# Accumulating depthwise taps in PSUM and splitting eight more gate strips, four by an adding DMA

## The chip, the cores and the metric

The kernel runs on one core of one Trainium2 chip. The metric is the device time of one execution in microseconds (us). The kernel before ran three times; one more execution was profiled.

## The reference

Two transformer-like blocks run one after the other on a sequence of 256 tokens with 1024 features, all in float32: retention and latent attention first, then a block with two mixers and a gated feed-forward part. The change lies in the mixer part of the second block:

```python
h = layer_norm(x) * (1.0 + sc1[:, None]) + sh1[:, None]
proj = h @ w_in[l]
a_val, a_gate, u_pool, gate_a, gate_b = jnp.split(
    proj, [COL_A_VAL, COL_A_GATE, COL_POOL, COL_GATE_A], axis=-1)
ya = a_val * jax.nn.sigmoid(a_gate)
ya = causal_dwconv(ya, w_dw_a[l], b_dw_a[l])          # 31 taps, 512 channels
ya = jax.nn.silu(layer_norm(ya, ln_a_g[l], ln_a_b[l]))
ya = ya @ w_pw_a[l]
pooled = causal_multiscale_pool(u_pool)               # windows 2, 4, 8, 16
...
merged = jax.nn.sigmoid(gate_a) * ya + jax.nn.sigmoid(gate_b) * yb
```

## The kernel before

**Weights and strips.** Every weight matrix is cut into blocks of 128 x 1024 (512 KB), numbered through the kernel (`B_WA` conv_in, 8 blocks; `B_WP` pool_in, 4; `B_WG` gates, 16; `B_POOL`, `B_PW` and so on). SyncE loads block b into slot b mod 4 of the ring `raw` (L337 to L373). A block that gives 128 output features for all 256 tokens is called a strip.

**Two ways to multiply.** A *split* strip needs two float32r copies of the block: the high part `whi`, a copy by ACT (`split`, L959 to L971), and the low part `wlo` = raw - whi, a subtract by VectorE (`split`, L1488 to L1495). Both work three blocks ahead of the call (`AHEAD`), and count up `hi_done` and `lo_done`. TensorE then makes three float32r products for each of eight 128 x 128 tiles (`products`, L469 to L481): high by high, high by low, low by high. A *native* strip (`plain_tokens`, L507) is multiplied in float32 straight from `raw`, with no copies; ACT and VectorE then raise `hi_done` and `lo_done` by a bare count (`skip_split`, L1040 and L1610), and SyncE waits for TensorE to be done with the slot (`load_plain`, `load_plain_loop`).

**The stage around the change.** TensorE runs conv_in (eight strips, three native and five split), pool_in (0 and 1 split, 2 and 3 native), gate strips 0 to 11 native, the matmul with ones for the convolution's mean (`conv_mean`, L596), then gate strips 12 to 15 split, with the matmul for its variance behind 13 (L902 to L920). Results of two strips share a bank: `GA[0]`, `GA[1]` in turn, evacuated by ACT with a sigmoid (`evac`, L1126). After the gates come the pooling product, the pointwise product of the convolution branch and the mixing product.

**The depthwise convolution** is VectorE's (L1966 to L2023). The gated values go into `CI`, four tiles of 128 channels with 30 zeros in front. Tap k of tile c is one `scalar_tensor_tensor` over 256 tokens: `CO[c] = CI[c, k:k+256] * w + CO[c]`, both tiles in SBUF; the first tap is a `tensor_scalar` with the bias. Each tap waits for the one before it in its tile (semaphore `conv_tap[c]`). 26 taps (four of them first taps) stand between the conv_in splits, 98 in a loop of seven passes of 14 taps. Two adds then form the channel sums (`CS`) for `conv_mean`; VectorE next makes the low parts of gate strips 12 and 13 and centres the result.

**The pooling** is GpSimd's (L2301 to L2312): once all four pool_in strips are evacuated into `U`, four windows one after the other, a few adds and two scalings each; ACT copies the result as a high part (L1372) behind a wait for all four.

The order of the work is written out by hand on every engine; each engine follows its own list, and semaphores tie them together.

Of the kernel before, what the change touches and what calls it, by code (L numbers as in the profile page):

```python
# [24 lines left out]
ALU = mybir.AluOpType  # L25
# [7 lines left out]
RING = 4  # L33
# [39 lines left out]
B_WP = B_WA + 8  # L73
# [11 lines left out]


KEPT = [B_PG0 + 4 + j for j in range(4)]


def raw_count(b):  # L90
# [34 lines left out]
def program(nc, x_in, pre_in, p_in, pos_in, cols_in, rows_in, mask_in, tri_in, cnt_in, ident_in, bias_in, ada_in, w, out):  # L125

    ctx = ExitStack()
    with ctx:
# [3 lines left out]
        def sem(name):  # L132
            return ctx.enter_context(nc.semaphore(name))
# [86 lines left out]
        bank = [PB[i // 2][:, 512 * (i % 2):512 * (i % 2) + 512] for i in range(8)]  # L220
        GA, GD = bank[0:2], bank[2:4]
        M0, M1, M2, M3 = bank[4:8]


        raw_loaded = [sem(f"raw_loaded{s}") for s in range(RING)]
        lo_done, hi_done, pe_done = sem("lo_done"), sem("hi_done"), sem("pe_done")
        act_free, dve_free = sem("act_free"), sem("dve_free")
        ada_loaded = [sem(f"ada_loaded{s}") for s in range(2)]
        plain_a, plain_d = sem("plain_a"), sem("plain_d")
        spare_loaded = [sem(f"spare_loaded{s}") for s in range(6)]  # L230
# [105 lines left out]
        def _(sp):  # L336
# [24 lines left out]
                    sp.wait_ge(pe_done, base + j + 1)  # L361
                    load(base + j, w[name][j], 1024)

            def load_plain_loop(base, name, count, per):

                with sp.Fori(0, count) as i:
                    for j in range(per):
                        sp.wait_ge(pe_done, base + j + 1 + per * i)
                        load(base + j, w[name][bass.ds(per * i + j, 1)].rearrange("b p n -> p (b n)"), 1024, per, i)

            def load_all(base, name):
                load_some(base, name, 0, w[name].shape[0])
# [70 lines left out]
            load_plain(B_WA, "conv_in", 6, 7)  # L443
            load_some(B_WA, "conv_in", 7, 8)
            load_all(B_WP, "pool_in")
            load_plain_loop(B_WG, "gates", 4, 4)
            load_all(B_POOL, "pool_w")
            load_all(B_PW, "pw")
            load_all(B_WO, "mix")
# [16 lines left out]
        def _(pe):  # L466
            mm = nc.tensor.matmul

            def products(base, parts, per=0, i=0, before=()):  # L469


                s = base % RING
                pe.wait_ge(lo_done, base + RING + 1 + per * i)
                for n, (t, a, o, start, stop) in enumerate(parts):
                    if n < len(before) and before[n]:
                        pe.wait_ge(*before[n])
                    c = slice(t * P, t * P + P)
                    mm(o, whi[:, s, c], a[:, 0, :], start=start, stop=False)  # L478
                    mm(o, whi[:, s, c], a[:, 1, :], start=False, stop=False)  # L479
                    last = mm(o, wlo[:, s, c], a[:, 0, :], start=False, stop=stop)  # L480
                last.then_inc(pe_done, 1)  # L481
# [38 lines left out]
            def free_a(k, per=0, i=0):  # L520

                pe.wait_ge(act_free, k + 1 + per * i)
                return GA[k % 2]
# [378 lines left out]
            for j in range(4):  # L902
# [3 lines left out]
                    strip(B_WP + j, halves(b)[j % 2], H)  # L906
                else:
                    plain_tokens(B_WP + j, halves(b)[j % 2])
            with pe.Fori(0, 3) as i:
                for j in range(4):  # L910
                    if j % 2 == 0:
                        b = free_a(A_WG + j // 2, 2, i)
                    plain_tokens(B_WG + j, halves(b)[j % 2], 4, i)
            conv_mean()
            for j in range(12, 16):
                if j % 2 == 0:
                    b = free_a(A_WG + j // 2)
                strip(B_WG + j, halves(b)[j % 2], H)
                if j == 13:
                    conv_squares()  # L920
            pe.wait_ge(pooled_ready, 1)
# [34 lines left out]
        def _(act):  # L956
            activation = nc.scalar.activation

            def split(base, n=1024, per=0, i=0):  # L959

                b = base + AHEAD
                if b >= B_END:
                    return
                s = b % RING
                if b in SPARE:
                    act.wait_ge(spare_loaded[SPARE[b]], spare_count(b))
                else:
                    act.wait_ge(raw_loaded[s], raw_count(b) + 16 * (per // RING) * i)
                if b not in KEPT:
                    act.wait_ge(pe_done, used_first(b) + per * i)  # L970
                activation(parts_of(b, n)[0], block_in(b, n), ACT.Copy).then_inc(hi_done, 1)  # L971

            def used(base, per=0, i=0):

# [62 lines left out]
                act.wait_ge(done, n)  # L1037
                activation(H[:, 4 * q:4 * q + 4, 0, tok(t)], zt[:, 4 * q:4 * q + 4, :], ACT.Copy).then_inc(turn_hi, 1)

            def skip_split(n):  # L1040

                activation(warm[:, 15:16], ones[:, 0:1], ACT.Copy).then_inc(hi_done, n)

            def dyn(a, t, n):
                return a[:, bass.ds(t, n), :]
# [314 lines left out]
            split(B_WA + 5)  # L1360
            value_gate(2)
            split(B_WA + 6)
            skip_split(14)
            value_gate(3)
            act.wait_ge(pads, 1)

            evac(B_WP + 1, 0, U[:, 0:2, 16:16 + T], ACT.Copy)
            evac(B_WP + 3, 1, U[:, 2:4, 16:16 + T], ACT.Copy)
            with act.Fori(0, 2) as i:
                evac(B_WG + 1, 0, dyn(G, 4 * i, 2), ACT.Sigmoid, 4, i)  # L1370
                evac(B_WG + 3, 1, dyn(G, 4 * i + 2, 2), ACT.Sigmoid, 4, i)
            act.wait_ge(pooled, 4)  # L1372
            activation(Sh, PO, ACT.Copy).then_inc(pooled_hi, 1)
            evac(B_WG + 9, 0, pair(G, 4), ACT.Sigmoid)
            for j in range(9, 12):
                split(B_WG + j)
# [106 lines left out]
        def _(dve):  # L1483
# [488 lines left out]
            def taps(c, ks, i=0, per=0):  # L1972

                for k in ks:
                    x = CI[:, c, bass.ds(k + per * i, T)]
                    w_tap = dcol("dwa", CONV_K * c + k + per * i)
                    if per == 0 and k == 0:
                        dve.wait_ge(dve_free, V_WA + c + 3)
                        ts(CO[:, c, :], x, w_tap, col("bdwa", c), ALU.mult, ALU.add).then_inc(conv_tap[c], 1)
                    else:  # L1980
                        dve.wait_ge(conv_tap[c], k + per * i)
                        stt(CO[:, c, :], x, w_tap, CO[:, c, :], ALU.mult, ALU.add).then_inc(conv_tap[c], 1)  # L1982

            split(B_WA)
            gated_value(0)
# [15 lines left out]
                taps(1, (3 + k,))  # L2001
                taps(2, (k,))
            split(B_WA + 6)
            skip_split(14)
            taps(0, (9,))
            for k in range(5, 10):
                taps(1, (k,))
# [1 line left out]
                    taps(2, (2,))  # L2009
            gated_value(3)  # L2010
            taps(3, (0, 1, 2))
            with dve.Fori(0, 7) as i:
                for k in range(4):
                    if k < 3:
                        taps(0, (10 + k,), i, 3)
                        taps(1, (10 + k,), i, 3)
                    taps(2, (3 + k,), i, 4)
                    taps(3, (3 + k,), i, 4)
            for c in range(4):
                dve.wait_ge(conv_tap[c], CONV_K)  # L2020
            tt(CS, pair(CO, 0), pair(CO, 1), ALU.add).then_inc(conv_sum, 1)
# [189 lines left out]
        def _(pool):  # L2211
# [86 lines left out]
            nc.gpsimd.memset(U[:, :, 0:16], 0.0).then_inc(pads, 1)  # L2298
            pool.wait_ge(pads, 1)

            pool.wait_ge(act_free, A_WP + 2 + 2)  # L2301
            for g, window in enumerate(WINDOWS):
                src, shift, n = U[:, g, :], 1, 0
                while shift < window:
                    lo = 2 * shift - 1
                    dst = W1[:, n % 2, :]
                    chained(gtt(dst[:, lo:16 + T], src[:, lo:16 + T], src[:, lo - shift:16 + T - shift], ALU.add))
                    src, shift, n = dst, 2 * shift, n + 1
                chained(gtt(src[:, 16:32], src[:, 16:32], cnt[:, g, :], ALU.mult))
                chained(gts(src[:, 16:16 + T], src[:, 16:16 + T], 1.0 / window, None, ALU.mult))  # L2310
                gtt(PO[:, g, :], src[:, 16:16 + T], U[:, g, 16:16 + T], ALU.subtract).then_inc(pooled, 1)
                pool.wait_ge(pooled, g + 1)  # L2312
# [123 lines left out]
```

## Time and profile before

| | us |
|---|---|
| median of 3 runs | 845.52 (844.92 to 847.47) |
| the profiled execution | 846.33 |
| its span in the profile | 844.5 |
| TensorE busy in the span | 831.2 |
| VectorE busy | 667.9 |
| ACT busy | 454.9 |
| GpSimd busy | 48.7 |

The span runs from the first to the last instruction; the execution's time is 1.83 us longer. Matmuls overlap, so that TensorE's busy time says where it worked, not how fast. Durations of neighbouring VectorE or ACT instructions overlap a little as well: the time from start to start is what such an instruction costs in a row of them. The granted TensorE clock was 1.00 in all stretches from 520 to 640 us.

### The profile page before, as it was taken

To read this page: it belongs to the slowest core of one execution; us is meant where nothing else is said; L and a number is where in the kernel's file an instruction comes from. 1 tells how busy PE (TensorE), PEld (TensorE's weight loads), DVE (VectorE), ACT (ScalarE), POOL (GpSimd) and SP (SyncE) were. 2 spreads that over 40 slices of the span, in tenths; PEclk is the share of its full clock that TensorE was granted. 3 is DMA by queue.
4 is the path that set the end of the run, shared out by engine and by line. 5 is a ranking of instruction groups with operands and counts; after the bars stand their busy time and mean duration, and the time that the engine had idled before them with its cause. 6 is when DMAs were issued, how large, how long until landed. Compare 5 with 4: busy or idle time off the path is not lost.

```text
span 844.5 us, 15113 instructions
## 1 busy us (share of the span) xinstructions
PE 831.2 (98%) x5434; PEld 759.5 (90%) x5434; DVE 667.9 (79%) x982; ACT 454.9 (54%) x680; POOL 48.7 (6%) x61
## 2 busy tenths in 40 slices
PE   9999999999999999999999999999999999999995
PEld 9899999988878999999988889988988999999884
DVE  7979888686966887787866777999898888788566
ACT  6464545554646665657555536102853867777440
POOL 0009000000012000000000000060000000000000
PEclk9999999999999999999999999999999999999998
DMA  7857565679634747383648562444662565566541
GB/s 271 303 196 246 204 243 200 223 252 379 226 102 162 263 137 264 114 286 124 243 149 329 196 224 97 133 152 157 219 219 99 199 204 188 179 193 229 187 164 50
DMA packets 48141, 168.98 MB, mean 200 GB/s; under 512 B 5602, under 2 KB 6242, under 8 KB 48100
## 3 DMA queue, kind: packets, MB, share of 16 engines
q1 hardware_dynamic: 40324, 142.18, 49.6%
q10 hardware_dynamic: 7776, 26.25, 8.7%
q8 instruction: 26, 0.43, 0.2%
q14 instruction: 15, 0.12, 0.0%
HBM read 167.36 MB, written 1.05 MB: 199 GB/s over the span
## 4 chain that ended last, share of the span: by engine, by line
PE 85%; DVE 8%; issue 3%; ACT 2%; DMA 1%; DVEq 1%; ACTq 0%
PE bank L478 13%; PE bank L479 12%; PE bank L480 12%; PE bank L545 9%; PE bank L547 9%; PE bank L546 9%; DVE WK L1982 4%; PE bank L491 3%; PE bank L696 2%; PE bank L697 2%; PE bank L698 2%; PE bank L588 1%; DVE wlo L1495 1%; PE bank L819 1%; PE bank L837 1%
## 5 line engine op out<-in xcount | busy, mean ns | idle before, releaser
L971 ACT ACTIVATE whi<-raw 128x1024 fp32r<-128x1024 f32 (+1 forms) x232 | 240.1, 1040 | 218.3 <-PE bank L480 95.3
L1495 DVE TENSOR_TENSOR wlo<-raw,whi 128x1024 fp32r<-128x1024 f32 (+1 forms) x232 | 278.5, 1212 | 79.7 <-ACT whi L971 77.1
L478 PE MATMUL bank<-H,whi 128*128 128x256 f32 x784 | 224.5, 286 | 0.5 <-DVE wlo L1495 0.5
L480 PE MATMUL bank<-H,wlo 128*128 128x256 f32 x784 | 221.8, 283 | 0.0
L479 PE MATMUL bank<-H,whi 128*128 128x256 f32 x784 | 221.7, 283 | 0.0
L478 PEld LDWEIGHTS bank<-H,whi 128*128 128x128 f32 x784 | 150.3, 192 | 1.8 <-issue 1.7
L479 PEld LDWEIGHTS bank<-H,whi 128*128 128x128 f32 x784 | 150.4, 192 | 0.1
L480 PEld LDWEIGHTS bank<-H,wlo 128*128 128x128 f32 x784 | 150.3, 192 | 0.0
L545 PE MATMUL bank<-whi,Y 128*128 128x512 f32 x216 | 84.3, 390 | 0.0
L547 PE MATMUL bank<-whi,Y 128*128 128x512 f32 x216 | 84.1, 389 | 0.0
L546 PE MATMUL bank<-wlo,Y 128*128 128x512 f32 x216 | 84.1, 389 | 0.0
L1511 DVE SCALAR_TENSOR_TENSOR ada_acc<-ada_raw,siluc,ada_acc 128x1024 f32<-128x1024 f32 x46 | 60.6, 1318 | 9.3 <-DMA ada_raw<-ada_in 8.1
L1982 DVE SCALAR_TENSOR_TENSOR WK<-WK,cols 128x256 f32<-128x256 f32 x120 | 55.8, 529 | 1.2 <-issue 0.2
L478 PE MATMUL bank<-Y,whi 128*128 128x256 f32 x176 | 50.6, 288 | 1.0 <-ACT G L1129 1.0
L480 PE MATMUL bank<-Y,wlo 128*128 128x256 f32 x176 | 49.8, 283 | 0.0
L479 PE MATMUL bank<-Y,whi 128*128 128x256 f32 x176 | 49.8, 283 | 0.0
L513 PE MATMUL bank<-Z,raw 128*128 128x256 f32 x224 | 48.5, 379 | 0.0
L547 PEld LDWEIGHTS bank<-whi,Y 128*128 128x128 f32 x216 | 40.5, 188 | 8.4
L545 PEld LDWEIGHTS bank<-whi,Y 128*128 128x128 f32 x216 | 40.5, 188 | 8.4
L546 PEld LDWEIGHTS bank<-wlo,Y 128*128 128x128 f32 x216 | 40.6, 188 | 8.3
L513 PEld LDWEIGHTS bank<-Z,raw 128*128 128x128 f32 x224 | 42.5, 190 | 5.7
L545 PE MATMUL bank<-whi,H 128*128 128x512 f32 x112 | 44.3, 395 | 0.0
(275 smaller groups left out, 1362.8 us busy)
## 6 DMA issues: line engine op xcount, KB each, us to landing
ada_raw<-ada_in ACTq DMA_DIRECT2D x48, 512.0 KB, 4.4
raw<-w_head SPq DMA_DIRECT2D x47, 512.0 KB, 4.4
raw<-w_up SPq DMA_DIRECT2D x42, 512.0 KB, 3.3
raw<-w_down SPq DMA_DIRECT2D x22, 512.0 KB, 4.2
raw<-w_uq SPq DMA_DIRECT2D x24, 384.0 KB, 3.1
raw<-w_ret_out SPq DMA_DIRECT2D x16, 512.0 KB, 5.6
raw<-w_mla_gate SPq DMA_DIRECT2D x16, 512.0 KB, 4.5
raw<-w_mla_out SPq DMA_DIRECT2D x16, 512.0 KB, 5.1
```

The costliest lines, as they stand in the source:

```text
L478: mm(o, whi[:, s, c], a[:, 0, :], start=start, stop=False)
L479: mm(o, whi[:, s, c], a[:, 1, :], start=False, stop=False)
L480: last = mm(o, wlo[:, s, c], a[:, 0, :], start=False, stop=stop)
L491: last = mm(o[:, tok(t)], raw[:, s, c], WT[:, t, c], start=(k == 0), stop=(k == 7))
L513: last = mm(o.rearrange("p (t m) -> p t m", t=2), raw[:, s, c], WT[:, :, c], start=(k == 0), stop=(k == 7))
L545: mm(o, a[:, k0 + k, 0, tok(t)], hi[:, c], start=start and k == 0, stop=False)
L546: mm(o, a[:, k0 + k, 0, tok(t)], lo[:, c], start=False, stop=False)
L547: last = mm(o, a[:, k0 + k, 1, tok(t)], hi[:, c], start=False, stop=stop and k == 1)
L971: activation(parts_of(b, n)[0], block_in(b, n), ACT.Copy).then_inc(hi_done, 1)
L1495: tt(lo, block_in(b, n), f32(hi), ALU.subtract).then_inc(lo_done, 1)
L1511: stt(ada_acc[:, a, :], ada_raw[:, n, :], siluc[:, bass.ds(2 * i + 2 * o + n, 1)], ada_acc[:, a, :] if before is None else before, ALU.mul ...
L1982: stt(CO[:, c, :], x, w_tap, CO[:, c, :], ALU.mult, ALU.add).then_inc(conv_tap[c], 1)
```

## The change

- The taps accumulate in `CT`, the 1024 columns of PSUM tensor `PB[2]` (two banks, four tiles of 256), in place of `CO`; only the last tap of each tile writes `CO`.
- Gate strips 0, 1, 4, 5 and 8 to 11 become split strips; 2, 3, 6 and 7 stay native. All gate loops are written out.
- For strips 8 to 11 VectorE makes the low part, between its last 28 taps, which leave the loop (five passes remain).
- For strips 0, 1, 4 and 5 (`ADDED`) ACT writes the high part and the negated high part into `wlo`, and a DMA issued by GpSimd reads the block from HBM once more and adds it onto `wlo`. TensorE waits for that transfer (`low_added`). GpSimd issues two before the pooling and one each before its second and third window.
- SyncE's loads follow: the slot of a copied block is free when ACT has copied it (`load_copied`).

```diff
+
+
+ADDED = {B_WG: 0, B_WG + 1: 1, B_WG + 4: 2, B_WG + 5: 3}
...
+        CT = PB[2][:].rearrange("p (c t) -> p c t", c=4)
...
+        low_added = [sem(f"low_added{n}") for n in range(len(ADDED))]
...
-            def load_plain_loop(base, name, count, per):
-
-                with sp.Fori(0, count) as i:
-                    for j in range(per):
-                        sp.wait_ge(pe_done, base + j + 1 + per * i)
-                        load(base + j, w[name][bass.ds(per * i + j, 1)].rearrange("b p n -> p (b n)"), 1024, per, i)
+            def load_copied(base, name, j0, j1):
+
+                for j in range(j0, j1):
+                    sp.wait_ge(hi_done, base + j + 1 - RING)
+                    load(base + j, w[name][j], 1024)
 
...
-            load_plain_loop(B_WG, "gates", 4, 4)
+            load_some(B_WG, "gates", 0, 2)
+            load_plain(B_WG, "gates", 2, 4)
+            load_copied(B_WG, "gates", 4, 6)
+            load_plain(B_WG, "gates", 6, 8)
+            load_copied(B_WG, "gates", 8, 10)
+            load_plain(B_WG, "gates", 10, 12)
+            load_some(B_WG, "gates", 12, 16)
...
-                pe.wait_ge(lo_done, base + RING + 1 + per * i)
+                if base in ADDED:
+                    pe.wait_ge(low_added[ADDED[base]], 16)
+                else:
+                    pe.wait_ge(lo_done, base + RING + 1 + per * i)
...
-            with pe.Fori(0, 3) as i:
-                for j in range(4):
-                    if j % 2 == 0:
-                        b = free_a(A_WG + j // 2, 2, i)
-                    plain_tokens(B_WG + j, halves(b)[j % 2], 4, i)
-            conv_mean()
-            for j in range(12, 16):
+            for j in range(16):
                 if j % 2 == 0:
                     b = free_a(A_WG + j // 2)
-                strip(B_WG + j, halves(b)[j % 2], H)
+                if j in (2, 3, 6, 7):
+                    plain_tokens(B_WG + j, halves(b)[j % 2])
+                else:
+                    strip(B_WG + j, halves(b)[j % 2], H)
+                if j == 11:
+                    conv_mean()
                 if j == 13:
                     conv_squares()
...
-                activation(parts_of(b, n)[0], block_in(b, n), ACT.Copy).then_inc(hi_done, 1)
+                hi, lo = parts_of(b, n)
+                if b in ADDED:
+                    activation(hi, block_in(b, n), ACT.Copy)
+                    activation(lo, block_in(b, n), ACT.Copy, scale=-1.0).then_inc(hi_done, 1)
+                else:
+                    activation(hi, block_in(b, n), ACT.Copy).then_inc(hi_done, 1)
...
-            def skip_split(n):
-
-                activation(warm[:, 15:16], ones[:, 0:1], ACT.Copy).then_inc(hi_done, n)
+            def skip_split(n, c=15):
+
+                activation(warm[:, c:c + 1], ones[:, 0:1], ACT.Copy).then_inc(hi_done, n)
...
-            skip_split(14)
+            skip_split(2)
             value_gate(3)
             act.wait_ge(pads, 1)
 
+            split(B_WP + 1)
             evac(B_WP + 1, 0, U[:, 0:2, 16:16 + T], ACT.Copy)
+            split(B_WP + 2)
+            skip_split(2, 14)
             evac(B_WP + 3, 1, U[:, 2:4, 16:16 + T], ACT.Copy)
-            with act.Fori(0, 2) as i:
-                evac(B_WG + 1, 0, dyn(G, 4 * i, 2), ACT.Sigmoid, 4, i)
-                evac(B_WG + 3, 1, dyn(G, 4 * i + 2, 2), ACT.Sigmoid, 4, i)
+            split(B_WG + 1)
+            evac(B_WG + 1, 0, pair(G, 0), ACT.Sigmoid)
+            split(B_WG + 2)
+            skip_split(2, 13)
+            evac(B_WG + 3, 1, pair(G, 1), ACT.Sigmoid)
+            split(B_WG + 5)
+            evac(B_WG + 5, 0, pair(G, 2), ACT.Sigmoid)
+            split(B_WG + 6)
             act.wait_ge(pooled, 4)
             activation(Sh, PO, ACT.Copy).then_inc(pooled_hi, 1)
+            split(B_WG + 7)
+            evac(B_WG + 7, 1, pair(G, 3), ACT.Sigmoid)
+            split(B_WG + 8)
             evac(B_WG + 9, 0, pair(G, 4), ACT.Sigmoid)
...
-                        ts(CO[:, c, :], x, w_tap, col("bdwa", c), ALU.mult, ALU.add).then_inc(conv_tap[c], 1)
+                        ts(CT[:, c, :], x, w_tap, col("bdwa", c), ALU.mult, ALU.add).then_inc(conv_tap[c], 1)
                     else:
                         dve.wait_ge(conv_tap[c], k + per * i)
-                        stt(CO[:, c, :], x, w_tap, CO[:, c, :], ALU.mult, ALU.add).then_inc(conv_tap[c], 1)
+                        total = CO if per == 0 and k == CONV_K - 1 else CT
+                        stt(total[:, c, :], x, w_tap, CT[:, c, :], ALU.mult, ALU.add).then_inc(conv_tap[c], 1)
...
-            skip_split(14)
+            skip_split(10)
...
-            with dve.Fori(0, 7) as i:
+            with dve.Fori(0, 5) as i:
                 for k in range(4):
                     if k < 3:
                         taps(0, (10 + k,), i, 3)
                         taps(1, (10 + k,), i, 3)
                     taps(2, (3 + k,), i, 4)
                     taps(3, (3 + k,), i, 4)
+
+            def last_taps(k0, k2, n):
+
+                for k in range(4):
+                    if k < 3:
+                        taps(0, (k0 + k,))
+                        taps(1, (k0 + k,))
+                    taps(2, (k2 + k,))
+                    taps(3, (k2 + k,))
+                    if k == 1 or (k == 3 and n == 6):
+                        split(B_WG + n + k // 2)
+
+            split(B_WG + 5)
+            last_taps(25, 23, 6)
+            last_taps(28, 27, 8)
...
+            def add_raw(j):
+
+                b = B_WG + j
+                pool.wait_ge(hi_done, b + 1)
+                nc.gpsimd.dma_start(wlo[:, b % RING, :], w["gates"][j], accum_op=ALU.add).then_inc(low_added[ADDED[b]], 16)
+
+            add_raw(0)
+            add_raw(1)
             pool.wait_ge(act_free, A_WP + 2 + 2)
             for g, window in enumerate(WINDOWS):
+                if g in (1, 2):
+                    add_raw(3 + g)
```

## Rows read from the trace of the kernel before

**Rows 1.** The page's first lines: span, busy time of each engine.
```profile
span 844.5 us, 15113 instructions
...
PE 831.2 (98%) x5434; PEld 759.5 (90%) x5434; DVE 667.9 (79%) x982; ACT 454.9 (54%) x680; POOL 48.7 (6%) x61
```

**Rows 2.** Busy time by stretch: start:end, length, then PE, PEld, DVE, ACT, POOL (instructions).
```profile
590.00:612.00 22.00, 21.01 (x170) 20.70 (x171) 18.71 (x23) 17.45 (x24) 0.00 (x0) 1.00 0.67 220
```

**Rows 3.** TensorE's timeline: start, length, line, operation, output and input [idle before, releaser].
```profile
520.32 0.28 PE L479 MATMUL bank<-H,whi 128*128 128x256 f32 x1
...
523.19 0.28 PE L479 MATMUL bank<-H,whi 128*128 128x256 f32 x1
...
540.35 48.51 PE L513 MATMUL bank<-Z,raw 128*128 128x256 f32 x224
...
588.86 0.67 PE L600 MATMUL bank<-WK,ones 128*128 128x256 f32 x2
...
590.00 0.36 PE L478 MATMUL bank<-H,whi 128*128 128x256 f32 x1 [0.47 <-DVE wlo L1495]
```

**Rows 4.** VectorE's timeline, 541 to 593 us.
```profile
541.18 5.63 DVE L1982 SCALAR_TENSOR_TENSOR WK<-WK,cols 128x256 f32<-128x256 f32 x14 [0.22 <-issue]
...
546.97 40.47 DVE L1982 SCALAR_TENSOR_TENSOR WK<-WK,cols 128x256 f32<-128x256 f32 x84
...
587.56 0.69 DVE L2021 TENSOR_TENSOR WK<-WK 128x512 f32<-128x512 f32 x1
...
588.29 0.42 DVE L2023 TENSOR_TENSOR WK<-WK 128x256 f32<-128x256 f32 x1
...
588.63 2.35 DVE L1495 TENSOR_TENSOR wlo<-raw,whi 128x1024 fp32r<-128x1024 f32 x2
...
592.10 1.22 DVE L1495 TENSOR_TENSOR wlo<-raw,whi 128x1024 fp32r<-128x1024 f32 x1
```

**Rows 5.** The chain in order of time: start, length, what; two loop passes.
```profile
568.07 1.00 DVE WK L1982 x3
...
573.83 1.00 DVE WK L1982 x3
```

**Rows 6.** GpSimd's timeline: first and last of the pooling, end of its first window.
```profile
548.20 0.94 POOL L2307 TENSOR_TENSOR WK<-WK 128x271 f32<-128x271 f32 x1 [28.47 <-ACT WK L1129]
...
550.62 0.72 POOL L2311 TENSOR_TENSOR ada_acc<-WK 128x256 f32<-128x256 f32 x1
...
564.28 0.81 POOL L2311 TENSOR_TENSOR ada_acc<-WK 128x256 f32<-128x256 f32 x1
```

**Rows 7.** Timelines of VectorE and GpSimd between 66 and 79 us.
```profile
66.88 0.68 DVE L1521 TENSOR_TENSOR WK<-bank,TAB 128x512 f32<-128x512 f32 x1
...
76.25 2.33 DVE L1495 TENSOR_TENSOR wlo<-raw,whi 128x1024 fp32r<-128x1024 f32 x1
...
66.41 1.91 POOL L2276 TENSOR_SCALAR G<-G 128x512 f32<-128x512 f32 x1
...
76.22 1.29 POOL L2280 TENSOR_TENSOR G<-G 128x512 f32<-128x512 f32 x1
```

**Rows 8.** VectorE's groups by form: count | busy us, mean ns | idle before.
```profile
L1521 DVE TENSOR_TENSOR WK<-bank,TAB 128x512 f32<-128x512 f32 x8 | 5.5, 682 | 0.0
...
L2064 DVE TENSOR_TENSOR Z<-Z,G 128x512 f32<-128x512 f32 x4 | 2.8, 692 | 0.1
...
L2031 DVE SCALAR_TENSOR_TENSOR G<-bank,cols,G 128x256 f32<-128x256 f32 x8 | 3.5, 477 | 0.0
```

**Rows 9.** VectorE's timeline, 608 us: two unlooped multiply-adds.
```profile
608.51 0.87 DVE L2031 SCALAR_TENSOR_TENSOR G<-bank,cols,G 128x256 f32<-128x256 f32 x2
```

**Rows 10.** The page's groups: ACT's high-part copies.
```profile
L971 ACT ACTIVATE whi<-raw 128x1024 fp32r<-128x1024 f32 (+1 forms) x232 | 240.1, 1040 | 218.3 <-PE bank L480 95.3
```

**Rows 11.** DMA issues: output, input, queue, count, KB each, median us to landing.
```profile
raw<-w_gates SPq DMA_DIRECT2D x16, 512.0 KB, 3.3
...
ada_raw<-w_up SPq DMA_DIRECT2D x2, 512.0 KB, 7.3
```

## The prediction

> **What bounds the kernel now.** The page's first part comes first: TensorE is busy in 831.2 of a span of 844.5 us, VectorE in 667.9, GpSimd in 48.7 [rows 1]. So TensorE sets the end almost everywhere, and an edit pays only where TensorE does less or waits less. The stage in question runs from 541 to 590 us: TensorE computes 14 native strips (two of pool_in, twelve gate strips) and VectorE the looped taps of the depthwise convolution. Three views show it. In the busy time by stretch, TensorE is busy in 21.01 of the 22 us after 590 [rows 2], so what it gains before that point it keeps. In TensorE's timeline the native matmuls end at 588.86, the mean of the convolution follows at once, and the next split strip starts at 590.00 after 0.47 us of waiting for its low part [rows 3]. In VectorE's timeline the 98 looped taps start at 541.18 and end at 587.56, the two adds behind them end at 588.71, 0.15 us before TensorE's mean matmul, and then come the low parts of strips 12 and 13 [rows 4]. So two engines finish this stage together. Relief on one alone gives next to nothing; what counts is the later of the two ends after the change.
>
> **TensorE's side.** The 14 native strips take 48.51 us, 3.465 each; 24 fp32r matmuls, one split strip, take 523.19 - 520.32 = 2.87, call it 2.88 [rows 3]. Eight strips change: 8 x 0.585 = 4.7 us less. If nothing else held it, TensorE would reach the mean at 588.86 - 4.7 = 584.2.
>
> **VectorE's side.** Without GpSimd one loop pass of 14 taps takes 573.83 - 568.07 = 5.76 us [rows 5]. Seven passes should take 40.3 and take 587.56 - 541.18 = 46.4, 6.0 more. The pooling on GpSimd runs exactly in between, 548.20 to 565.09 [rows 6]. That this is contention for SBUF, and that an accumulator in PSUM escapes it, shows earlier in the trace [rows 7]: with a GpSimd instruction beside it, a subtract of two SBUF tiles takes 2.33 us at 76.25, where two such together take 2.35 at 588.63 [rows 4], while a product of a PSUM bank with one SBUF tile takes 0.68 at 66.88, its mean over the whole span [rows 8]. After the change a tap reads one SBUF tile (CI) and one bank (CT). I take the whole 6.0 us as gone. Ends: nothing gone (0), all gone (6.0).
>
> Added on VectorE: four low parts (strips 8 to 11), at the cadence of the pair at 588.63 less one duration, that at 592.10: 2.35 - 1.22 = 1.13 us each [rows 4]: +4.5. The other four new low parts cost it nothing. Its 28 last taps leave the loop: 5.76/14 = 0.411 us becomes 0.87 - 0.477 = 0.393, the cadence of the same operation unlooped [rows 8, 9]: -0.5. A larger skip count and the last tap's output into CO cost nothing: the instruction was there already.
>
> The unknown is a VectorE output into PSUM, which no row has. For the input, the rows with a bank as a source are not slower: 682 against 692 ns at 512 elements, and 477 at 256 elements with a bank [rows 8]. At worst a tap cannot start before the one in front has wholly ended, 477 in place of 393 ns: +84 ns, over 98 taps +8.2 us. At best it gets so cheap that VectorE drops out, and TensorE's 4.7 us are the limit. I take 0, the nearest rows being those with a bank as input. The Trainium skill, Perfetto Trace Analysis, Optimizing Scalar/DVE Operations, speaks against the change: it puts VectorE's overhead at about 60 ns on SBUF and 125 on PSUM. By that the 98 taps would be 6.4 us dearer and the kernel some 4.4 slower; the input side of the rule this trace does not bear out (682 against 692 ns).
>
> Sum for VectorE: -6.0 + 4.5 - 0.5 = **-2.0 us**, so the adds end at 586.7.
>
> **Do the pieces fit?** TensorE reaches gate strip 0 at 547.3, then 1 at 550.2, 2 at 553.0, 3 at 556.5, 4 at 560.0, 5 at 562.9, 6 at 565.7, 7 at 569.2, 8 at 572.7. VectorE ends five passes at 570.0 and has strip 8's low part at 571.2, in time; strip 9's after 8 more taps at 575.5, just in time; strip 10's at 579.0 against 578.4 (0.6 us wait); strip 11's at 583.3 against 582.0 (1.3 us wait). TensorE ends strip 11 at 586.2, before the adds at 586.7. VectorE alone ends the stage, and TensorE idles some 3 us in it. Behind it the same low parts, square root and Silu follow in the same order, so the 2.0 us carry through.
>
> **ACT.** Twelve added copies of about 1.04 us [rows 10] (eight high, four negated) and two more one-element skips. ACT mostly waits for TensorE here. For strips 0 and 1 it waits until the pool strips with their ring slots are done (537.5 and 540.4), then copies twice: hi_done at 539.7, and after the evacuation of pool_in's first pair at about 543.3. In front of evacuations these copies hold nothing: strip 4 needs the evacuation behind strip 1's wait only at 560.0.
>
> **SyncE.** In its order strip 4's load stands behind strip 3's wait (TensorE at 547.3), so it lands near 551.1 at 3.3 us [rows 11]; ACT's copies end by 553.3. Strips 8 and 9 stand behind 7's wait (560.0), land by 564.5, wanted as high parts before 571. Strips 10 and 11 wait for TensorE (569.2, 572.7), land by 576.1, high part by 577.2, wanted at 582. No load is late.
>
> **GpSimd and the adding transfers.** Nobody's compute does the four low parts; 2 MB are read from HBM a second time. GpSimd now waits for ACT's copy of strip 4 before its second window: it is free at 551.3 [rows 6] and goes on at 553.3. Behind that stand three windows and ACT's copy of the pooled tile, and behind that in turn ACT's strips 10 and 11; pooling ends near 568 to 569, and strip 10 has its raw tile only at 572.6. Hidden, with some 3 us to spare. Time between the copy and TensorE's need: strip 0 7.6 us, strip 1 6.9, strip 4 6.7, strip 5 (issued after the second window, near 557.5) 5.4. A plain load of this size lands in 3.3 us, the slow ones in 7.3 [rows 11]. Price between 0 (3.3) and, at 7.3, TensorE 1.9 us late, which its 2.5 us of spare (586.7 - 584.2) still hides. I take 0. The Trainium skill, DMA: Bandwidth & Descriptors, Anatomy of one DMA, fits GpSimd-issued DMAs with 2.0 us plus bytes/436e3: 3.2 us here by estimate, and no figure for adding ones; by it nothing would be late either.
>
> **Against the measurement.** The profiled execution took 846.33 us, 1.83 around its span. It would become 844.3. It is 0.81 above the median of the runs, 845.52, and the prediction on that basis is **843.5**. About 0.3%, 2.5 us, is what a measurement here can tell from no change: below 843.0 is faster, above 848.1 slower.
>
> **Rivals.**
> 1. *Taps into PSUM are cheaper, TensorE ends the stage.* From 26 ns less per tap (2.5/98) VectorE is done before 584.2. Time 845.5 - 4.7 = 840.8. For: output and accumulator leave SBUF altogether. Against: the 256-element cadence is the same with a bank as input. Chance 0.13.
> 2. *Taps into PSUM are dearer*: each tap's start waits for the bank write of the one in front. Place: the 98 taps from 541 on. Break-even at 20 ns (2.0/98); at 42 ns a tap 847.6, at 84 ns 851.7. Against: the input rows. For: no row has the output. Chance 0.17, three quarters of it beyond 848.1. By the rule of the Trainium skill, Perfetto Trace Analysis, Optimizing Scalar/DVE Operations, 65 ns a tap, it would be 849.9.
> 3. *The adding transfers are late.* The transfer reads its destination, adds and writes back, and GpSimd must issue it. It takes from the gain beyond 7.9 us between strip 5's issue and its landing (5.4 + 2.5), and loses from 10.1 (5.4 + 4.7). At twice the slow load, 14.6 us, TensorE is 9.2 late and comes to the mean at 584.2 + 9.2 = 593.4, 4.5 later than now: 850.0. Its signature is TensorE waiting at gate strips 0, 1, 4 or 5. Chance 0.15.
> 4. *The change doesn't relieve VectorE as meant:* half of the 6.0 us stays, since the per-channel weight is still read from SBUF. 843.5 + 3.0 = 846.5. Chance 0.10; the bank products in rows 7 have no such weight.
>
> The forecast itself has 0.45, with a spread of 842.4 to 844.6 (cadence of the unlooped taps, 0.3 us at the stage's edge). About four tenths of it lies below 843.0. Faster: 0.18 + 0.13, rounded up to 0.33. Slower: rival 3 with 0.14 and three quarters of rival 2, 0.13, together 0.27. Same: 0.40. The range goes down to rival 1 at 840.8 and up to 849.8, into rivals 2 and 3.
>
> **What the new profile would show.** Right: tap rows of 477 ns in all stretches, no stretching beside GpSimd; native matmul rows down from 224 to 96; the adds about 2.0 us earlier, VectorE without idle time from 541 to 587; TensorE waiting for L1495's low parts at strips 10 and 11 and for the sum at the mean, some 3 us. Wrong if tap rows are longer or shorter by over 20 ns, if TensorE waits on a DMA into wlo, or if the part behind 590 does not move as a block.

## The result, and the profile after

The changed kernel took 849.20 us (median of 14 runs, 847.57 to 851.22), the kernel before, measured along with it, 845.58 (14 runs, 844.92 to 847.97): ratio 1.0037 [1.0029, 1.0045], 3.6 us slower, where 843.5 was forecast. The profiled execution took 849.33.

The page's first lines, against [rows 1]:

```profile
span 847.5 us, 15137 instructions
PE 827.7 (98%) x5498; PEld 759.1 (90%) x5498; DVE 665.9 (79%) x986; ACT 467.5 (55%) x694; POOL 51.1 (6%) x65
```

TensorE is 3.5 us less busy and the span 3.0 longer: it waits more. Busy time by stretch (start:end, length, then PE, PEld, DVE, ACT, POOL with their instructions, granted clock, DMA share, GB/s) says where:

```profile
548.00:565.00 17.00, 14.08 (x88) 12.52 (x87) 16.55 (x43) 5.07 (x7) 10.75 (x16) 1.00 0.77 212
565.00:590.00 25.00, 20.86 (x129) 20.03 (x130) 19.41 (x42) 8.76 (x10) 3.80 (x7) 0.86 0.49 171
590.00:612.00 22.00, 21.17 (x172) 20.80 (x171) 18.45 (x22) 17.76 (x24) 0.00 (x0) 1.00 0.55 177
```

TensorE idles 2.9 us in the first stretch and 4.1 in the second, and there the granted clock is 0.86; before, it was 1.00 in the whole stage. Behind 590 TensorE is as busy as in [rows 2] (21.17 us of 22, before 21.01). TensorE's timeline, with the idle time before an instruction and its releaser in brackets:

```profile
539.00 7.07 PE L526 MATMUL bank<-Z,raw 128*128 128x256 f32 x32
...
549.45 0.39 PE L491 MATMUL bank<-H,whi 128*128 128x256 f32 x1 [0.52 <-DMA wlo<-w_gates]
...
559.90 0.35 PE L491 MATMUL bank<-H,whi 128*128 128x256 f32 x1 [0.40 <-DMA wlo<-w_gates]
...
562.72 0.28 PE L493 MATMUL bank<-H,wlo 128*128 128x256 f32 x1
569.14 0.58 PE L491 MATMUL bank<-H,whi 128*128 128x256 f32 x1 [6.14 <-DMA wlo<-w_gates]
569.52 0.41 PE L492 MATMUL bank<-H,whi 128*128 128x256 f32 x1
569.74 0.41 PE L493 MATMUL bank<-H,wlo 128*128 128x256 f32 x1
569.95 0.41 PE L491 MATMUL bank<-H,whi 128*128 128x256 f32 x1
...
574.37 7.07 PE L526 MATMUL bank<-Z,raw 128*128 128x256 f32 x32
...
592.79 0.59 PE L613 MATMUL bank<-WK,ones 128*128 128x256 f32 x2
```

The three waits are for the adding transfers of strips 1, 4 and 5. The last takes 6.14 us, and the strip behind it has a cadence of 0.21 us a matmul in place of 0.12: 569.14 to 574.37 = 5.2 us in place of 2.9. The same in two stretches cut at this strip:

```profile
569.14:574.37 5.23, 5.23 (x25) 5.23 (x25) 3.08 (x6) 1.06 (x1) 0.14 (x1) 0.51 0.02 9
574.37:592.00 17.63, 17.63 (x124) 16.80 (x123) 14.33 (x30) 8.77 (x10) 0.00 (x0) 1.00 0.50 180
```

The clock was 0.51 for that one strip, the 1.2 GHz level, and back at 2.4 GHz behind it. It had fallen while TensorE still waited; it was 1.00 up to 567 us, 0.72 from 567 to 568 and 0.50 from 568 to 569.14, and over the whole wait:

```profile
562.70:569.14 6.44, 0.30 (x3) 0.10 (x1) 5.98 (x16) 0.00 (x0) 5.79 (x9) 0.87 0.95 290
```

From 569.14 on TensorE works without a gap, so it alone sets the mean matmul at 592.79. The stage from the first native pool_in strip to the mean takes 592.79 - 539.00 = 53.8 us, before 588.86 - 540.35 = 48.5 [rows 3]: 5.3 longer. From the mean to the end of the span it is 847.5 - 592.79 = 254.7, before 844.5 - 588.86 = 255.6: 0.9 given back, half of it the 0.47 us wait for a low part at 590.00, which is gone. And the stage began 1.35 us earlier. 5.3 - 0.9 - 1.35 = 3.0, the difference of the spans. The start of the stage lies between 538.9 and 541.4 in the 13 profiles of this study, kernels with the same code ahead of it among them; stage lengths are compared from here on.

The chain of waits that leads to strip 5 (start, length, what):

```profile
546.52 5.47 DMA raw<-w_gates
552.01 0.64 ACT whi L985
...
552.98 1.05 ACT wlo L986
...
554.57 0.91 POOL wlo L2349
...
558.21 0.74 POOL ada_acc L2365
...
559.24 9.86 DMA wlo<-w_gates
569.14 0.58 PE bank L491
```

DMA in the window 559.8 to 569.1 (issues: KB each, median us to landing):

```profile
q1 hardware_dynamic: 505, 1.81, 63.9%
q0 software_dynamic: 144, 0.52, 30.2%
...
raw<-w_gates SPq DMA_DIRECT2D x3, 512.0 KB, 10.2
wlo<-w_gates POOLq DMA_DIRECT2D x1, 512.0 KB, 9.9
```

Strip 5's transfer took 9.9 us and SyncE's loads beside it 10.2, against a median of 3.3 before [rows 11]. Taken one at a time, the four adding transfers (strips 0, 1, 4, 5) took 6.3, 7.4, 5.2 and 9.9 us.

VectorE's timeline:

```profile
540.31 5.58 DVE L2011 SCALAR_TENSOR_TENSOR bank<-WK,cols,bank 128x256 f32<-128x256 f32 x14 [0.21 <-issue]
546.05 5.58 DVE L2011 SCALAR_TENSOR_TENSOR bank<-WK,cols,bank 128x256 f32<-128x256 f32 x14 [0.16 <-issue]
551.80 17.03 DVE L2011 SCALAR_TENSOR_TENSOR bank<-WK,cols,bank 128x256 f32<-128x256 f32 x42 [0.16 <-issue]
571.29 1.23 DVE L1523 TENSOR_TENSOR wlo<-raw,whi 128x1024 fp32r<-128x1024 f32 x1 [2.46 <-ACT whi L988]
...
582.37 1.23 DVE L1523 TENSOR_TENSOR wlo<-raw,whi 128x1024 fp32r<-128x1024 f32 x1 [2.65 <-ACT whi L988]
...
591.07 0.43 DVE L2067 TENSOR_TENSOR WK<-WK 128x256 f32<-128x256 f32 x1
```

The 42 taps of three passes take 17.03 us beside GpSimd's pooling, 5.7 us a pass: nothing is stretched any more. From the loop's start to the end of the adds it is 591.50 - 540.31 = 51.2 us, before 588.71 - 541.18 = 47.5 [rows 4]; 5.6 of it are waits for ACT's copies (2.46, 0.49, 2.65), which themselves wait for loads. VectorE is done 1.3 us before the mean matmul, so these waits do not set the end here.

### The profile page after: what moved, and what is told of

It reads as the page before. It is cut to its first block, busy times and chain, and to the rows that moved or that the text cites. A ratio compares the mean times of both kernels' runs of the same rounds, so it can differ in the third digit from the quotient of the medians.

```text
span 847.5 us, 15137 instructions
## 1 busy us (share of the span) xinstructions
PE 827.7 (98%) x5498; PEld 759.1 (90%) x5498; DVE 665.9 (79%) x986; ACT 467.5 (55%) x694; POOL 51.1 (6%) x65
## 4 chain that ended last, share of the span: by engine, by line
PE 92%; DVE 3%; DMA 2%; ACT 2%; issue 0%; POOL 0%; SPq 0%; ACTq 0%; DVEq 0%; POOLq 0%
PE bank L491 15%; PE bank L492 14%; PE bank L493 14%; PE bank L558 9%; PE bank L559 9%; PE bank L560 9%; PE bank L504 3%; PE bank L709 2%; PE bank L710 2%; PE bank L711 2%; PE bank L526 2%; PE bank L601 1%; DMA wlo<-w_gates 1%; PE bank L832 1%; PE bank L850 1%; PE bank L628 1%
## 5 line engine op out<-in xcount | busy, mean ns | idle before, releaser
L988 ACT ACTIVATE whi<-raw 128x1024 fp32r<-128x1024 f32 (+1 forms) x236 | 244.5, 1041 | 229.4 <-PE bank L493 93.6
L1523 DVE TENSOR_TENSOR wlo<-raw,whi 128x1024 fp32r<-128x1024 f32 (+1 forms) x236 | 283.2, 1212 | 82.2 <-ACT whi L988 80.4
L491 PE MATMUL bank<-H,whi 128*128 128x256 f32 x848 | 244.5, 288 | 7.1 <-DMA wlo<-w_gates 7.1
L492 PE MATMUL bank<-H,whi 128*128 128x256 f32 x848 | 240.9, 284 | 0.0
L493 PE MATMUL bank<-H,wlo 128*128 128x256 f32 x848 | 240.8, 284 | 0.0
L491 PEld LDWEIGHTS bank<-H,whi 128*128 128x128 f32 x848 | 163.6, 193 | 8.9 <-DMA wlo<-w_gates 7.1
L492 PEld LDWEIGHTS bank<-H,whi 128*128 128x128 f32 x848 | 163.7, 193 | 0.2
L493 PEld LDWEIGHTS bank<-H,wlo 128*128 128x128 f32 x848 | 163.6, 193 | 0.0
L1539 DVE SCALAR_TENSOR_TENSOR ada_acc<-ada_raw,siluc,ada_acc 128x1024 f32<-128x1024 f32 x46 | 60.6, 1318 | 11.3 <-DMA ada_raw<-ada_in 10.1
L2011 DVE SCALAR_TENSOR_TENSOR bank<-WK,cols,bank 128x256 f32<-128x256 f32 x116 | 47.8, 483 | 1.2 <-issue 0.5
L558 PE MATMUL bank<-whi,H 128*128 128x512 f32 x112 | 44.3, 395 | 0.0
L560 PE MATMUL bank<-whi,H 128*128 128x512 f32 x112 | 43.7, 390 | 0.0
L559 PE MATMUL bank<-wlo,H 128*128 128x512 f32 x112 | 43.6, 389 | 0.0
```

The costliest lines, as they stand in the source:

```text
L558: mm(o, a[:, k0 + k, 0, tok(t)], hi[:, c], start=start and k == 0, stop=False)
L559: mm(o, a[:, k0 + k, 0, tok(t)], lo[:, c], start=False, stop=False)
L560: last = mm(o, a[:, k0 + k, 1, tok(t)], hi[:, c], start=False, stop=stop and k == 1)
L988: activation(hi, block_in(b, n), ACT.Copy).then_inc(hi_done, 1)
L1523: tt(lo, block_in(b, n), f32(hi), ALU.subtract).then_inc(lo_done, 1)
L1539: stt(ada_acc[:, a, :], ada_raw[:, n, :], siluc[:, bass.ds(2 * i + 2 * o + n, 1)], ada_acc[:, a, :] if before is None else before, ALU.mul ...
```

## Experiments

Two theories. **A:** the loss is the adding transfers: they land too late for TensorE. **B:** it lies in VectorE's part (taps into PSUM, four more low parts), and the wait is an accident beside it. The unchanged kernel had medians of 846.0, 845.9 and 845.81 us in the three batches of runs (1 to 4; 5 to 8; 9 to 11). Each batch ran on another chip, and a run's distance from the change differs by up to 1.2 us between medians and ratios (each ratio is to the unchanged kernel of its own batch). Small differences from the change are therefore read from the stage lengths in the traces.

### 1. The adding transfers taken out

```diff
-ADDED = {B_WG: 0, B_WG + 1: 1, B_WG + 4: 2, B_WG + 5: 3}
+ADDED = {}
-                if j in (2, 3, 6, 7):
+                if j < 8:
```

(with ACT's copies for 0, 1, 4 and 5 and `add_raw` taken out, and the loads of `load_plain`)

> Keeps the taps in PSUM and the four split strips whose low parts VectorE makes (8 to 11); gate strips 0, 1, 4 and 5 are native again and the four adding transfers are gone. Theory A (the adding transfers are late, and slow SyncE's loads beside them): the forecast's sum holds for what is left: TensorE 4 x 0.585 = 2.3 us less, VectorE 2.0 us less, so 842.5 to 844 us, the adds of the convolution near 586.7, no TensorE wait for wlo over 1.5 us. Theory B (what costs is VectorE: four low parts between the taps and its waits for them): no better than before, 845.5 to 848.

Measured: 843.21 us, 0.9960 [0.9947, 0.9974], inside the range of theory A. No wait on a transfer. The stage takes 586.64 - 540.60 = 46.0 us, and 10 x 3.465 + 4 x 2.88 = 46.2 is TensorE's own work. VectorE, from its loop's start to the end of the adds, takes 586.26 - 540.69 = 45.6, 2.0 less than before. Rows of VectorE's timeline:

```profile
540.69 5.58 DVE L2000 SCALAR_TENSOR_TENSOR bank<-WK,cols,bank 128x256 f32<-128x256 f32 x14 [0.22 <-issue]
...
585.84 0.42 DVE L2056 TENSOR_TENSOR WK<-WK 128x256 f32<-128x256 f32 x1
```

B falls: VectorE's whole part of the change is in this kernel, and it is faster than before.

### 2. The taps alone

```diff
-                        stt(CO[:, c, :], x, w_tap, CO[:, c, :], ALU.mult, ALU.add)
+                        total = CO if per == 0 and k == CONV_K - 1 else CT
+                        stt(total[:, c, :], x, w_tap, CT[:, c, :], ALU.mult, ALU.add)
```

(made in the kernel before, together with the first tap and the last loop pass written out; all twelve gate strips stay native)

> The kernel before with the taps in PSUM alone; the last loop pass is written out because the last tap writes CO; all twelve gate strips stay native. Theory A: taps keep 477 to 482 ns beside GpSimd, the adds end some 6 us earlier, TensorE's native strips still end near 588.9, and the only gain is that strip 12 no longer waits for its low part after the mean: 0.5 to 1.1 us, 844.5 to 845.2. Theory B with dearer taps: 845.6 or more.

Measured: 845.73 us, 0.9993 [0.9980, 1.0007]. The adds end 580.29 - 539.29 = 41.0 us after the loop's start, 6.5 earlier than before, and nothing comes of it: TensorE needs 587.63 - 539.28 = 48.35 for its 14 native strips. Relief on VectorE alone is worth nothing.

The median missed the 844.5 to 845.2 that were expected, and lies where dearer taps were expected. But its ratio leaves no difference from the unchanged kernel of its batch (846.0), the taps last 480 ns (median), and the adds end early: dearer taps are out. TensorE's wait for strip 12's low part is gone, and the 0.5 to 1.1 us expected from that did not show in the time.

### 3. The change with the taps left in SBUF

```diff
-        CT = PB[2][:].rearrange("p (c t) -> p c t", c=4)
+        CT = WK[:, 16:20, :]
```

> The change with the accumulator CT laid over the SBUF tile CO in place of the PSUM banks, everything else as in the change. Theory A: the taps stretch again beside GpSimd, some 6 us more on VectorE, of which up to 5.6 us fill the waits it has for ACT's copies in the change; since TensorE is late there by itself, 849 to 853 us. Rival (PSUM taps are a cause of the loss): faster than the change, below 848.

Measured: 850.88 us, 1.0049 [1.0031, 1.0066]: 1.7 above the change in the medians, 1.0 by the ratios, whose intervals overlap. The stage takes 594.67 - 539.37 = 55.3 us, 1.5 more than in the change. VectorE's timeline, passes 2 and 3 to 5:

```profile
545.18 6.66 DVE L2011 SCALAR_TENSOR_TENSOR WK<-WK,cols 128x256 f32<-128x256 f32 x14 [0.15 <-issue]
552.00 22.79 DVE L2011 SCALAR_TENSOR_TENSOR WK<-WK,cols 128x256 f32<-128x256 f32 x42 [0.16 <-issue]
```

The first takes 6.66 us in place of 5.58, the other three 22.79 where the bank takes 17.03: 6.8 us more in these four passes, the contention with GpSimd. Some of it fits into the 5.6 us that VectorE waits in the change anyway, so only some 1.5 show. PSUM taps are no cause of the loss. The wait at strip 5 is there with either kind of tap, a little longer here, its transfer being issued 22.0 us after the stage's start in place of 20.2:

```profile
570.58 0.58 PE L491 MATMUL bank<-H,whi 128*128 128x256 f32 x1 [6.91 <-DMA wlo<-w_gates]
```

### 4. The same transfers without the addition

The transfer overwrites `wlo` in place of adding, so these four low parts are the raw block and the kernel's output is not the reference's; its work and its order are those of the change.

```diff
-nc.gpsimd.dma_start(wlo[:, b % RING, :], w["gates"][j], accum_op=ALU.add)
+nc.gpsimd.dma_start(wlo[:, b % RING, :], w["gates"][j].bitcast(F32R))
```

> The change with the same four transfers issued by GpSimd at the same places, but overwriting wlo instead of adding (the low part of strips 0, 1, 4 and 5 is then the raw block and not raw minus high). If the adding is what makes them slow: 3.3 to 5 us from issue to landing in place of 5.2 to 9.9, TensorE's wait at strip 5 below 4 us, 844 to 847 us. If the issue on GpSimd and the sharing of the DMA engines with SyncE's loads make them slow: landing times within 1.5 us of the change's, 848 to 850 us.

Measured: 843.64 us, 0.9972 [0.9960, 0.9984], a little below the range given. Same bytes read from HBM, same queue, same places in the order; the four land in 3.7, 3.7 and at most 4.4 us (least, median, most). All that is left of TensorE's waits on a transfer:

```profile
563.94 0.39 PE L491 MATMUL bank<-H,whi 128*128 128x256 f32 x1 [0.89 <-DMA wlo<-w_gates]
```

The granted clock is 1.00 throughout. VectorE takes 586.03 - 540.43 = 45.6 us again. DMA from 535 to 612 us, first in the change, then here:

```profile
q0 software_dynamic: 576, 2.10, 15.4%
```

```profile
q0 software_dynamic: 576, 2.10, 9.1%
```

For the same 2.10 MB in 576 packets the adding transfers occupy the DMA engines 1.7 times as long. So what costs is the adding form of the transfer, not the second read of the block, nor GpSimd's queue. (The edit also names the block float32r, as `wlo` is, where the change reads it as float32; no run separates this from the addition.) GpSimd's issue instruction is shorter too: 0.54 to 0.81 us, against 0.87 to 1.09 with the addition.

### 5. Only strips 0 and 1 by an adding transfer, 4 and 5 native

```diff
-ADDED = {B_WG: 0, B_WG + 1: 1, B_WG + 4: 2, B_WG + 5: 3}
+ADDED = {B_WG: 0, B_WG + 1: 1}
```

(and strips 4 and 5 native on TensorE, SyncE and ACT)

> The change with adding transfers for strips 0 and 1 only; 4 and 5 are native. Theory A (lateness, with the clock's fall behind it, is the whole loss): in the change strip 1 makes TensorE wait 0.5 us only, so this kernel is limited by VectorE again: 843 to 844.5 us. Rival (an adding transfer costs by itself, wherever it stands, some 1.4 us each): 846 or more.

Measured: 843.77 us, 0.9977 [0.9966, 0.9987]; one wait for a transfer, 0.50 us at strip 1. The stage takes 585.37 - 539.68 = 45.7. The loss sits with strips 4 and 5; an adding transfer does not cost by its mere presence.

### 6. Strip 5's transfer issued right behind strip 4's

```diff
-                if g in (1, 2):
-                    add_raw(3 + g)
+                if g == 1:
+                    add_raw(4)
+                    add_raw(5)
```

> The change with strip 5's transfer issued right behind strip 4's, before GpSimd's second pooling window, some 2.8 us earlier. If the place of the issue makes strip 5 late: TensorE's wait there falls from 6.1 us to 2.5 to 4, and the time by as much, 845.5 to 847.5. If the transfers slow one another down by as much as the earlier issue wins: wait of 5 us or more, 848.5 to 849.5.

Measured: 843.96 us, 0.9978 [0.9966, 0.9989]. The issue comes at 556.28, the transfer takes 8.6 us, directly behind the other and beside three loads of 7.4. TensorE's wait, and the stretch that had 0.86:

```profile
564.91 0.38 PE L491 MATMUL bank<-H,whi 128*128 128x256 f32 x1 [2.27 <-DMA wlo<-w_gates]
```

```profile
565.00:590.00 25.00, 25.00 (x182) 24.11 (x183) 23.93 (x46) 12.56 (x15) 5.29 (x7) 1.00 0.54 194
```

2.27 us of idle time in place of 6.14, and the clock stays at 2.4 GHz. Wait and time are both better than expected (2.5 to 4 us, 845.5 to 847.5); the expectation had left out what the clock gives back. Issuing 3.0 us earlier shortens the stage from 53.8 to 586.30 - 538.93 = 47.4 us and wins 5.2 in the medians.

### 7. The low parts by a GpSimd subtract

```diff
-nc.gpsimd.dma_start(wlo[:, b % RING, :], w["gates"][j], accum_op=ALU.add)
+gtt(wlo[:, b % RING, :], raw[:, b % RING, :], f32(whi[:, b % RING, :]), ALU.subtract)
```

(ACT makes only the high part; the load behind waits for the subtract)

> The change with the low parts of strips 0, 1, 4 and 5 made by a GpSimd subtract of raw and high part (no negated copy, no second read of the block); SyncE's loads into these slots wait for that subtract. By the rows of the pooling I expect 2.5 to 3 us for one. Theory A: all four in time, no wait of TensorE over 1 us at these strips, VectorE limits, 843 to 844.2 us. Rival (splitting these four strips doesn't pay whoever makes the low part): above 845.

Measured: 843.68 us, 0.9966 [0.9952, 0.9980]. The four subtracts take 2.36 to 2.39 us each, in the places where the issues stood:

```profile
559.28 2.39 POOL L2348 TENSOR_TENSOR wlo<-raw,whi 128x1024 fp32r<-128x1024 f32 x1
```

TensorE waits for no transfer and for none of these; it waits 0.38 us for VectorE's low part of strip 10, 1.07 for that of strip 11 and 0.59 for the sum: VectorE sets the end.

```profile
582.76 0.39 PE L491 MATMUL bank<-H,whi 128*128 128x256 f32 x1 [1.07 <-DVE wlo L1522]
...
586.49 0.67 PE L613 MATMUL bank<-WK,ones 128*128 128x256 f32 x2 [0.59 <-DVE WK L2066]
```

### 8. SyncE's loads held until strip 5's transfer has landed

```diff
+            sp.wait_ge(low_added[3], 16)
             load_copied(B_WG, "gates", 8, 10)
```

> The change with one more wait on SyncE: the load of strip 8 and all behind it start only when strip 5's adding transfer has landed. If SyncE's loads on the same DMA engines stretch that transfer: from issue to landing 5.2 to 7.5 us in place of 9.9, TensorE's wait at strip 5 below 4.5 us; the time falls by less, since strips 8 and 9 now come later, 846 to 849. If not: landing 9 us or more, the wait stays near 6 us, 849.5 or more.

Measured: 849.18 us, 1.0034 [1.0020, 1.0049]: no better than the change in the time, though the stage of the profiled execution is 1.3 us shorter (591.92 - 539.40 = 52.5). Neither expectation holds whole: the wait of 4.83 us and the landing of 8.9 lie between them. Strip 5's transfer takes 8.9 us in place of 9.9, with two loads beside it in place of three:

```profile
568.41 0.58 PE L492 MATMUL bank<-H,whi 128*128 128x256 f32 x1 [4.83 <-DMA wlo<-w_gates]
...
569.01 0.41 PE L494 MATMUL bank<-H,wlo 128*128 128x256 f32 x1
```

One load less beside it is worth 1 us, not the 4 to 5 by which 9.9 exceeds the 5.2 of strip 4's. How much the two loads that stay add is not shown. The clock fell here too (0.53 from 568.41 to 573.50). And the load held back comes late: VectorE waits 4.89 us for strip 8's high part, at 572.86.

### 9. TensorE kept busy ahead of strip 5

```diff
+                if j == 5:
+                    hold(M2, 24)
```

(24 matmuls of ones into a free bank; the profile lists each in two rows)

> The change with 24 matmuls of ones by ones into an unused bank in front of strip 5; 14 such matmuls take 3.3 us in the kernel before, so these fill some 5.7 us of the 6.1 that TensorE waits there. The transfer is as late as before. If the fall of the granted clock behind the wait costs what the rows say (strip 5 in 5.4 us where a split strip takes 2.9): the strip at full clock, TensorE some 2.5 us earlier, 846 to 847.5 us. If the clock costs nothing in the end: 848.5 to 849.5.

Measured: 847.34 us, 1.0029 [1.0013, 1.0045]: 1.9 below the change in the medians, 0.7 by the ratios, whose intervals overlap. So the time alone does not show the gain; the trace does. TensorE's timeline:

```profile
563.63 5.52 PE L594 MATMUL bank<-ones 128*128 128x128 f32 x48
570.50 0.39 PE L491 MATMUL bank<-H,whi 128*128 128x256 f32 x1 [1.34 <-DMA wlo<-w_gates]
```

Strip 5 now takes 3.0 us at a granted clock of 1.00, though its transfer landed as late as ever (10.7 us after the issue). The stage takes 591.89 - 539.72 = 52.2 us, 1.6 less than in the change: 2.2 won in strip 5 itself, which starts 0.6 later in its stage (30.8 us against 30.1). So in the traces about 2 us of the loss are the slow clock, and the rest is lateness itself.

### 10 and 11. A version that beats both

Run 7 ends at VectorE. So of its eight added splits VectorE loses one (strip 11 native), or two (10 and 11 native):

```diff
-                if j in (2, 3, 6, 7):
+                if j in (2, 3, 6, 7, 10, 11):
```

(of the version with two; with the loads, copies and bare counts of these strips as for a native one)

> The kernel with GpSimd's low parts (strips 0, 1, 4, 5), and strip 11 native: VectorE makes three low parts (8, 9, 10) in place of four. VectorE gains 1.13 us, TensorE loses 0.585, and VectorE was the later by some 2: 842.2 to 843.3 us, 0.5 to 1.1 faster than with four. If something else than VectorE held that kernel: no gain, 843.7 or more.

> As the one before, with strip 10 native as well: two low parts on VectorE (8, 9), six strips split in all. TensorE's side now limits: native strips end 6 x 0.585 = 3.5 us earlier than before, VectorE 6.5 - 2.3 = 4.3 earlier; 841.8 to 842.9 us. If splitting pays no more from here: as with three low parts, or slower.

Measured: 842.71 us, 0.9964 [0.9952, 0.9977] with one; **841.64 us, 0.9958 [0.9945, 0.9971]** with two, the first inside its range, the second 0.2 below it. TensorE's mean matmul with two:

```profile
586.32 0.59 PE L614 MATMUL bank<-WK,ones 128*128 128x256 f32 x2
```

The stage takes 586.32 - 541.43 = 44.9 us, what eight native and six split strips need (8 x 3.465 + 6 x 2.88 = 45.0). VectorE is done at 584.71. With one, TensorE needs 44.4 and the stage takes 584.26 - 539.29 = 45.0; it waits 0.21 us for the sum. The two stages are equally long; the medians differ by 1.1 us, the ratios by 0.5, and the two intervals overlap, so which of the two is faster is open. Both are faster than the kernel before and the change.

## Why the prediction was wrong

**What failed is one step, "GpSimd and the adding transfers", with "No load is late" beside it.** The step priced an adding transfer by plain loads, 3.3 us and at the slow end 7.3 [rows 11], and so put its cost at 0. Measured were 5.2 to 9.9 us, and the same transfers without the addition 3.7 to 4.4 (run 4). The slow end was itself too low: 7.3 is a median, and between 500 and 640 us of the kernel before the slowest plain load took 7.9. The text's own rival 3 named this mechanism and its signature, with 0.15.

In figures, from the start of the stage: strip 5's issue was forecast at 557.5 - 540.35 = 17.2 us and came at 559.24 - 539.00 = 20.2. Of these 3.1 us, 2.2 are strip 4's load: issued on time, it took 5.5 us instead of 3.3, beside strip 1's adding transfer and other loads. The rest is in ACT's copies and GpSimd's issue. But the forecast of the issue was too early without any addition as well: in run 4 this load took 4.6 us and the issue came at 559.53 - 540.45 = 19.1, 1.9 late, and TensorE still waited 0.89 us at strip 5. The landing added 9.9 - 3.3 = 6.6. Together 9.7 late, against the 2.1 between forecast landing (557.5 + 3.3) and need (562.9); and TensorE itself was 1.3 later, by 0.9 for strips 1 and 4. 9.7 - 2.1 - 1.3 = 6.3: the gap from 562.84 to 569.14.

**What rival 3 lacked.** It counted from the issue, which it took as on time, and by its bounds a transfer of 9.9 us would only just have used up the gain (a loss from 10.1). And it counted lateness alone. The clock fell during the wait and made strip 5 take 5.2 us instead of 2.9. TensorE's own work of 43.8 us (6 x 3.465 + 8 x 2.88) plus gaps of 0.64, 0.55 and 6.30 us ahead of strips 1, 4 and 5, plus 5.23 - 2.88 = 2.35 for the clock is 53.6; measured 53.8.

**What held.**
- VectorE's sum, -2.0 us: -1.9 and -2.0 in runs 4 and 1. A pass takes 551.80 - 546.05 = 5.75 us beside GpSimd, forecast 5.76; a low part has a cadence of 1.14, forecast 1.13. The contention is gone whole; half of it staying (rival 4) is excluded.
- The price of 0 for an output into PSUM. A tap lasts 482 ns (median) with the bank on both sides and 477 with its output in SBUF, at the same cadence. Rivals 1 and 2 are out. By the Trainium skill, Perfetto Trace Analysis, Optimizing Scalar/DVE Operations, a tap would by estimate have been 65 ns dearer; the passes of 14 taps (5.75 us with the bank, 5.76 without) show nothing of it.
- TensorE's 0.585 us per split strip: run 1 has 46.0 where the sum gives 46.2, run 11 has 44.9 for 45.0.
- "Relief on one alone gives next to nothing": run 2.
- The forecast of 2.0 us less (843.5) is what comes out where low parts are not late or hardly so: 2.4 below the unchanged kernel of the same batch in run 4, 1.9 in run 6, 2.2 in run 7. In run 6 it is in part luck: there TensorE, with 2.27 us of waiting, ends the stage and not VectorE.

The 0.5 us wait of TensorE at strip 1 and 0.4 at strip 4 belong to the same step: the time given to them, 6.9 and 6.7 us, was about what the transfers took (7.4 and 5.2, the latter issued late).

**Open.** Why the adding form makes a transfer slow was not tried, nor what each of its neighbours adds: run 8 took one load of three away and won 1 us, run 6 has 8.6 us with another adding transfer directly ahead.

## What to carry to other kernels

Price a kind of transfer that the trace does not have by a run of it, not by rows of another kind, and take its effect on the loads beside it into the sum: here both ate a slack of 2 us. Before work is moved onto a queue that is issued between other work, look how early it can be issued; 3 us there were worth 5 here, the clock's share among them. Where two engines end a stage together, move work between them until neither waits for the other; runs 10 and 11 do this with the help of an engine that was mostly idle.

## What was not expected of the hardware

- An adding transfer of 512 KB of float32 from HBM onto SBUF took 5.2 to 9.9 us (10.7 in run 9), a plain one from the same queue 3.7 to 4.4. The Trainium skill, DMA: Bandwidth & Descriptors, Anatomy of one DMA, gives by its fit an estimate of 3.2 us for plain ones, without a figure for adding ones; run 4 is 0.5 to 1.2 above it.
- TensorE's granted clock fell to the 1.2 GHz level for one strip with 6.14 us of waiting ahead of it, and so with 6.91 (run 3) and 4.83 (run 8); with 2.27 it did not (run 6), nor when the gap was filled with matmuls (run 9). In the change the fall came before the wait was over.
- The first tap, a multiply and add with two scalars, lasts 0.55 us into a bank and 0.41 into SBUF; for the taps behind it there is no such difference.
- A GpSimd subtract of 128 x 1024 float32 takes 2.36 us, about two of VectorE's, and did not slow the taps once their accumulator was in PSUM.
